# A slot table and the order of VectorE's work in the two mixer stages of a two-layer transformer kernel

## The reference, cut to what matters

```python
# block 1: mixer M0
q_a, k_a, v_a, q_b, k_b, v_b, g_a, g_b = split(rms(x) @ w_in)
y_a = moba_attention(rotary(q_a), rotary(k_a), v_a)       # 8 softmax heads
y_b = stick_breaking_attention(q_b, k_b, v_b)             # 8 heads, log-sigmoid sums
merged = sigmoid(g_a + b) * (y_a @ w_branch_moba) + sigmoid(g_b + b) * (y_b @ w_branch_sb)
x = x + merged @ w_out
# block 2: mixer M1
fq, fk, fv, ff, dq, dk, dv, iq, ik, iw, ga, gb = split(rms(x) @ w_in_2)
o_a = fox_attention(norm(fq), norm(fk), fv, log_sigmoid(ff + b_forget))   # 8 heads
score = sum_h iw[h] * relu(iq[h] . ik)                    # 8 index heads
sel = top_k(causal(score), 64)
o_b = dsa_attention(norm(dq), norm(dk), dv, sel, rel_bias)                # 8 heads
merged = sigmoid(ga) * (o_a @ w_branch_a) + sigmoid(gb) * (o_b @ w_branch_b)
x = x + merged @ w_out_2
```

## Time and profile before

| | us |
|---|---|
| median of three runs | 1149.95 (1149.85 to 1151.63) |
| the profiled execution's own time | 1151.63 |
| its span, first to last instruction | 1149.8 |
| PE busy | 1132.0 (98% of the span) |
| DVE busy | 691.5 (60%) |
| ACT busy | 577.7 (50%) |
| POOL busy | 66.0 (6%) |
| mean granted TensorE clock | 0.997 |

### The profile page before, as it was taken

The page is one execution under the profiler, slowest core; times in us unless marked ns, Lnnn a source line. Parts: engine busy times, 40 slices in busy tenths (PEclk is TensorE's granted clock), DMA queues, the critical chain, the costliest instruction groups (busy, mean ns, idle before and its releaser), DMA issues.

```text
span 1149.8 us, 13571 instructions
## 1 busy us (share of the span) xinstructions
PE 1132.0 (98%) x5422; PEld 943.1 (82%) x5422; DVE 691.5 (60%) x869; ACT 577.7 (50%) x714; POOL 66.0 (6%) x106
## 2 busy tenths in 40 slices
PE   8999999999999999999999999999899999999998
PEld 6888888888888888888888888888688888888887
DVE  5555554654887765555485555457995486555542
ACT  4444442667656444444354445337667764444440
POOL 2000000100000000000000000030344200000000
PEclk8999999999999999999999999999999999999999
DMA  9656566644445566555565555556634355555550
GB/s 310 224 183 186 184 225 214 200 164 144 141 174 176 172 201 191 184 192 183 183 201 183 184 183 183 195 164 239 201 112 146 127 168 180 186 183 183 183 183 37
DMA packets 143039, 208.53 MB, mean 181 GB/s; under 512 B 9336, under 2 KB 100616, under 8 KB 142976
## 3 DMA queue, kind: packets, MB, share of 16 engines
q1 hardware_dynamic: 139296, 198.01, 52.7%
q0 software_dynamic: 3248, 9.06, 2.3%
q10 hardware_dynamic: 432, 0.59, 0.2%
HBM read 206.56 MB, written 2.64 MB: 182 GB/s over the span
## 4 chain that ended last, share of the span: by engine, by line
PE 90%; DVE 4%; ACT 3%; issue 1%; DMA 1%; SPq 0%; ACTq 0%; DVEq 0%
PE bank L1526 28%; PE bank L1528 27%; PE bank L1527 27%; PE bank L1635 2%; DVE w_lo L1041 2%; DMA raw<-in_ffn_w_up 1%; ACT w_hi L710 1%; PE bank L1548 1%; PE bank L1765 1%; PE bank L1792 1%; PE bank L1793 1%; DVE stat L1406 1%; PE bank L1791 0%; PE bank L1752 0%; DVE gate L1364 0%
## 5 line engine op out<-in xcount | busy, mean ns | idle before, releaser
L1041 DVE TENSOR_TENSOR w_lo<-raw,w_hi 128x2048 fp32r<-128x2048 f32 (+1 forms) x187 | 426.1, 2283 | 215.5 <-ACT w_hi L710 215.2
L1526 PE MATMUL bank<-w_hi,xT_hi 128*128 128x512 f32 (+1 forms) x1112 | 440.1, 396 | 1.8 <-DVE xT_lo L1061 1.8
L1528 PE MATMUL bank<-w_hi,xT_lo 128*128 128x512 f32 (+1 forms) x1112 | 432.9, 389 | 0.0
L1527 PE MATMUL bank<-w_lo,xT_hi 128*128 128x512 f32 (+1 forms) x1112 | 431.9, 388 | 0.0
L710 ACT ACTIVATE w_hi<-raw 128x2048 fp32r<-128x2048 f32 (+1 forms) x187 | 354.7, 1901 | 109.2 <-PE bank L1528 105.1
L1528 PEld LDWEIGHTS bank<-w_hi,xT_lo 128*128 128x128 f32 x1112 | 209.1, 188 | 44.5
L1526 PEld LDWEIGHTS bank<-w_hi,xT_hi 128*128 128x128 f32 x1112 | 209.4, 188 | 41.1 <-DVE w_lo L1041 2.0
L1527 PEld LDWEIGHTS bank<-w_lo,xT_hi 128*128 128x128 f32 x1112 | 209.7, 189 | 39.7
L1526 PE MATMUL bank<-w_hi,hT_hi 128*128 128x512 f32 x352 | 137.7, 391 | 0.0
L1528 PE MATMUL bank<-w_hi,hT_lo 128*128 128x512 f32 x352 | 137.1, 389 | 0.0
L1527 PE MATMUL bank<-w_lo,hT_hi 128*128 128x512 f32 x352 | 137.0, 389 | 0.0
(11 more groups left out here) (274 smaller groups left out, 780.7 us busy)
## 6 DMA issues: line engine op xcount, KB each, us to landing
raw<-in_ffn_w_gate SPq DMA_DIRECT2D x88, 512.0 KB, 4.0
raw<-in_ffn_w_up SPq DMA_DIRECT2D x88, 512.0 KB, 5.0
raw<-in_ffn_w_down SPq DMA_DIRECT2D x88, 512.0 KB, 4.2
raw<-in_w_in SPq DMA_DIRECT2D x76, 512.0 KB, 4.5
raw<-in_w_out SPq DMA_DIRECT2D x16, 512.0 KB, 4.0
raw<-in_w_branch_moba SPq DMA_DIRECT2D x4, 512.0 KB, 5.0
raw<-in_w_branch_sb SPq DMA_DIRECT2D x4, 512.0 KB, 6.0
raw<-in_w_branch_a SPq DMA_DIRECT2D x4, 512.0 KB, 4.5
```

The costliest lines, as they stand in the source:

```text
L1041: dve.tensor_tensor(w_lo[r][:, 0:n], raw[r][:, 0:n], w_hi[u % SLOTS][:, 0:n], ALU.subtract).then_inc(lo_done, 1)
L1526: pe.matmul(dst, st(hi), mhi, start=start, stop=False)
L1527: pe.matmul(dst, st(hi), mlo, start=False, stop=False)
L1528: return pe.matmul(dst, st(lo), mhi, start=False, stop=stop)
```

## The change

The edit moves work between slots and within a slot. No instruction on data is added or taken away by the source. For M0 the DVE part of each slot now has `gate_rows` first and `sb_keep` behind the `split_lo`. For M1 the index heads stand one per slot at 10 to 17 and their `accumulate` is two slots after the scores, ahead of the split. The transposes of fk and fq come up to two slots later and in another order, dk's at slot 28, the fox heads at 21 and 23 to 29, dq's at 30 and 31, and the dsa heads at 32 to 39. The second `norm_heads` moves to slot 19, `norm_dk` to 18, the top rounds to slots 20 to 27, `select` to 28 and 29.

```diff
-        out = [(6, "TR", ("iq", 0)), (7, "TR", ("iq", 1)), (9, "TR", ("ik", 0)), (12, "CU", ())]
-        out += [(t, "IX", h) for h, t in enumerate((10, 10, 11, 11, 12, 13, 13, 14))]
-        out += [(16, "TR", ("fq", 0)), (17, "TR", ("dk", 0)), (18, "TR", ("fq", 1))]
-        out += [(19, "TR", ("fk", 0)), (20, "TR", ("fk", 1))]
-        out += [(t, "SM", ("fox", h)) for h, t in enumerate((21, 22, 23, 24, 25, 26, 27, 28))]
-        out += [(29, "TR", ("dq", 0)), (30, "TR", ("dq", 1))]
-        out += [(t, "SM", ("dsa", h)) for h, t in enumerate((31, 32, 33, 34, 35, 36, 37, 38))]
+        out = [(6, "TR", ("iq", 0)), (7, "TR", ("iq", 1)), (9, "TR", ("ik", 0)), (11, "CU", ())]
+        out += [(10 + h, "IX", h) for h in range(NH)]
+        out += [(18, "TR", ("fq", 0)), (19, "TR", ("fk", 0)), (20, "TR", ("fq", 1)), (22, "TR", ("fk", 1))]
+        out += [(t, "SM", ("fox", h)) for h, t in enumerate((21, 23, 24, 25, 26, 27, 28, 29))]
+        out += [(28, "TR", ("dk", 0)), (30, "TR", ("dq", 0)), (31, "TR", ("dq", 1))]
+        out += [(t, "SM", ("dsa", h)) for h, t in enumerate((32, 33, 34, 35, 36, 37, 38, 39))]
...
-                rounds = {17 + k: k for k in range(TOPK // 8)}
+                rounds = {20 + k: k for k in range(TOPK // 8)}
...
+                    if b == 0 and q == 0 and 7 <= j <= 10:
+                        dve.wait_ge(tri_done, 1)
+                        gate_rows(j - 1)
                     for it in ITEMS[b]:
...
-                        if it.kind == "SB" and d == SB_AT["keep"]:
-                            sb_keep(it)
                         if it.kind == "SM" and d == SM_AT["out"]:
                             invert(it)
-                    if b == 0 and q == 0 and 7 <= j <= 10:
-                        dve.wait_ge(tri_done, 1)
-                        gate_rows(j - 1)
+                        if it.kind == "IX" and d == 2:
+                            accumulate(it)
...
-                        if slot == 16:
-                            norm_heads(0)
-                            norm_dk()
+                        if slot in (16, 19):
+                            norm_heads((slot - 16) // 3)
                     if q in (1, 3) and 1 < slot < 42:
                         for u in next_units(ph, j)[q // 2:q // 2 + 1]:
                             split_lo(u)
...
                         if slot == 18:
-                            norm_heads(1)
+                            norm_dk()
...
-                        if it.kind == "IX" and d == 1:
-                            accumulate(it)
+                        if it.kind == "SB" and d == SB_AT["keep"]:
+                            sb_keep(it)
...
-                    if b == 1 and slot in (25, 26):
-                        select(slot - 25)
+                    if b == 1 and slot in (28, 29):
+                        select(slot - 28)
```

## The result

The changed kernel takes 1156.82 us (median of 4 runs, 1155.52 to 1158.11) where the kernel before takes 1150.02 (median of 4, 1149.85 to 1151.63). The ratio is 1.0056, with a 95% interval of 1.0038 to 1.0074: some 6.4 us (0.0056 x 1150) slower. The profiled execution took 1156.88, with a span of 1155.1. The forecast was 1154.5 within 1150.8 to 1157.6, slower with a chance of 0.70.

A forecast was written before the change was run, and what follows sets the result against it. The prediction took PE to bound the kernel. M0 +3.8 and M1 -3.8 + 4.5 = +0.7 gave +4.5 us, taking the median from 1149.95 to 1154.5; own range 1153.0 to 1156.3, 8-in-10 range 1150.8 to 1157.6.

The forecast's parts named there:

- M0, DVE and ACT queues: M0's first two stick-breaking heads: the new order makes PE wait 1.4, then 2.4 us, together 3.8 us later.
- M1 body: M1, index heads to fox heads: PE's waits shrink from 6.9 to 3.5 us; gain taken as 3.8.
- M1 tail: End of M1: the last dsa head's exponentials fall behind the Sigmoid preload, adding two table loads; 4.5 us lost.
- the first step: M0, first head: keep behind the split makes PE's sum wait and the next scores start 1.4 us later.
- its step: M0, second head: `gate_rows` ahead of the clamp delays softplus and `w_hi`; PE's second sum waits 2.3 to 2.4 us more.
- Up to 816 us the spread work fits in gaps: M1: the index heads' accumulates stand where DVE waited for `w_hi`; DVE's last idle moment is at 816.2.
- the walk: M1: DVE's queue followed by row durations from 816.2, 28.1 us of work, to fk1's `turn_rest` ending at 844.3.
- Missing loads: Rival, M1's tail: the table loads don't come or don't hold PE; tail loses 1.9, total 1151.9; chance 0.15.
- M0's first step only: Rival, M0: the order costs only its first step, 1.4 us, total 1152.1; chance 0.10.
- a cleared backlog: Rival, M1: DVE's backlog clears wholly, 1146.8, or 1149.4 with loads; chance 0.10 under 1147.6, otherwise 0.05.
- M1 gains nothing: Rival, M1: the stalls don't shrink at all, total 1158.2; chance 0.10.
- the last two rivals: M1's stalls don't shrink, 1158.2, chance 0.10; a table load costs the page's price, 1157.3, chance 0.03.

The follow-up runs named there:

- after_again: The changed kernel itself, unaltered, executed once more for a second trace: 1156.79 us.
- m0_keep_only: The kernel before with only M0's `sb_keep` moved behind the split, `gate_rows` left in its old place: ratio 1.0019 to the kernel before.
- m1_part_no_masks: The changed kernel with M0's old order put back and each of POOL's eight masks cut to one column: ratio 1.0001 to the kernel before.
- m1_dsa_early_2: The kernel of m1_dsa_early run again, unaltered: ratio 0.9985 to the kernel before.
- m1_one_load: The changed kernel with M0's old order and M1's Sigmoid preload moved from slot 40 to behind slot 41's exponentials: ratio 0.9993 to the kernel before.
- m0_part_only: The kernel before with both M0 moves (`gate_rows` first, `sb_keep` behind the split) and M1 as before: ratio 1.0045 to the kernel before.
- m1_dsa_early: The changed kernel with M0's old order, and dq's transposes and the dsa heads at their old slots: ratio 0.9988 to the kernel before.
- the kept-busy kernel: m0_part_only with useless matmuls on PE ahead of the first two sums, their results overwritten: ratio 1.0032 to the kernel before.
- m0_gate_only: The kernel before with only M0's `gate_rows` moved ahead of the items, `sb_keep` left ahead of the split: ratio 1.0023 to the kernel before.
- m1_early_dk_late: m1_dsa_early with `norm_dk` moved to slot 24, behind fox's four transposes: ratio 0.9997 to the kernel before.

## Why the prediction was right, and where it was off

| step | forecast | measured in the trace after |
|---|---|---|
| M0, DVE and ACT queues | +3.8 | +3.82 (3.75 in after_again) |
| M0, clock | none | +1.6 here, 0 in after_again |
| M1 body | -3.8 | -2.95 |
| M1 tail | +4.5 | +4.6 |
| sum | +4.5 | +7.05 |

The measured 1156.82 lies inside the stated range, but 0.5 above the forecast's own 1153.0 to 1156.3. Part of the nearness is luck: the profiled execution, forecast at 1156.1, took 1156.88 because it started 1.8 us early; with before's start the same work would have ended at 1151.63 + 7.05 = 1158.7.

**M0's queues: right.** The second sum stands 311.25 - 309.25 + 1.82 = 3.82 later, for the start's 1.82. Of the first step, 0.97 was forecast for the first sum, and 0.97 it was. More than half of the third wait is the doing of `gate_rows`, as its step said: counted from the first sum, the second keep ends at 311.15 - 300.83 = 10.3 in the changed kernel and at 309.84 - 300.84 = 9.0 in m0_keep_only, with `gate_rows` back in its place. That m0_keep_only shows no third wait at all is the slow clock's doing.

**M0's clock: missing.** No term of the sum stood for what PE's clock does behind a wait. Before, PE has no waits over 0.3 us in this stretch, and in M1, where it has four of 0.9 to 2.3, the clock is 1.00 in that trace: from there I could read that waits are harmless, and read it too generally. That the waits bring the fall is shown: in all six traces with new waits in M0 the clock fell there once, and in the other eight, with M0's old order or with PE kept busy in the first and third wait, it stayed at 1.00. This is the largest error, 1.6 us.

**M1's body: the mechanism right, the size off.** POOL's masks do "start some 4 us earlier" and "are over by then": they end ahead of `norm_dk`. The step that failed is "Up to 816 us the spread work fits in gaps", with DVE's last idle moment at 816.2. It priced the masks for `norm_dk` alone and left everything that they now fell on at its old duration. They start 3.8 us earlier against PE's work (16.67 us after the first index scores, in place of 20.44), but `norm_heads` of slot 16 is only 1.6 us earlier (17.06 in place of 18.67). It had run ahead of the masks and now runs among them: 4.3 us (814.91 to 819.19) in place of 1.85. `norm_dk` escaped them, as forecast (0.65, near the lower bound of 0.7), and the rest was hit: the accumulate 1.71 in place of 0.74, the split 2.71. So the contention moved and did not go. DVE has no idle moment there, and the split of slot 17 starts at 820.93 - 3.53 = 817.40 on before's scale, 1.2 us after the walk's 816.2 (3.53 is how much later M1's first index scores stand in this trace); without the masks, in m1_part_no_masks, it starts at 816.6 on that scale. The waits add up to 4.2 (0.35, 1.81, 0.43, 1.61) where 3.5 was forecast, and fk0's, forecast at 0.5, is the one that is off. The end of fk1's `turn_rest` is at 848.91 - 3.53 = 845.4, 1.1 us later than the 844.3 of the walk; no wait followed it, where 0.4 was forecast. m1_part_no_masks gives 1.2 us back, and m1_dsa_early_2 shows what else it hangs on: there the DMA that feeds the masks landed a microsecond later, the 128x18 instructions kept their 0.18, and fk0's wait was 1.06 where the same kernel had 1.92.

The Trainium skill (SBUF — State Buffer, section "SBUF: two separate sides") says that a GpSimd operation and a DVE operation with two SBUF inputs exclude each other on a shared port pair, for the whole instruction. The rows fit: a DVE instruction of 0.18 with two such inputs takes up to 0.67 beside masks of 0.87 each, and in m1_dsa_early_2 the reduce with one input (820.72, 1.21 us) keeps its time beside masks that run to 822.09. By that rule, overlap with POOL should have been priced for every DVE instruction with two SBUF inputs in the masks' 7 us, not for `norm_dk` alone.

**M1's tail: right.** The 4.6 of the table is 16.09 - 10.61 less the 0.85 of PE's work that the forecast also took off, and the body is what is left of M1's 1.7. Three loads, PE's waits before the last turn (1.83, "about 2") and before `y_turn` (2.40, "2 to 3"), +16.09 where +15.95 was forecast. The drain that the Trainium skill (ScalarE: Activation LUTs, section "What ACT_TABLE_LOAD costs") gives for a load does not show: 917.31 follows 916.01 + 1.28 at once, as the earlier trace rows showed, and m1_one_load's 2.86 for two loads leaves 0.15 each for all that is around them.

**The rivals.** Missing loads, M0's first step only, and a cleared backlog are all excluded by the trace. That M1 gains nothing is excluded too, though the body gained 0.85 less. The total came nearer to the last two rivals (1158.2 and 1157.3) than to the forecast, but for another reason than theirs, mostly the clock: M1's waits did shrink, and two loads cost 2.86, hardly more than 2 x 1.28.

**Still open.** What decides where the clock falls. In M0 it fell behind the same three waits at one of two places. In M1 it fell in five of the fourteen traces, each time about the first of the longer waits (1.9 to 2.3 us): in m0_part_only and m0_keep_only, whose M1 is that of the kernel before, in after_again, m1_one_load and m1_dsa_early. It cost nothing there (interval B 127.34 and 127.38 in the first two, where before has 127.34), since more waits follow. No kernel here was made to find what sets it. The price by run times alone is not sharp either: the kept-busy kernel's 1.5 us lies within the two intervals, and it is the traces (intervals A of 497.02 and 495.42 for one kernel, 495.48 with PE kept busy) that carry it.

## What to carry to other kernels

Walk each queue with the rows' durations: the walk gave M0's queues and the tail to 0.15 us. Then ask two more questions of it: which of the moved instructions now lie under another engine's work on the same memory, and whether a new wait of a microsecond or two on an otherwise full PE is followed by a stretch at half clock. An operation on an in-order list that switches a table belongs behind the last user of the old table, and a half that gains should be kept when the other loses: here M1's new order with the dsa heads and M0 left alone runs at 0.9985 to 0.9988 of the kernel before, the best of all that ran: a gain of 1.4 to 1.7 us, small, with intervals that end just under 1.

## What the runs showed of the hardware

- PE's granted clock fell to 0.50 behind two waits of 0.80 and 0.71 us (m0_keep_only, after_again), behind a further one of 2.17 (after, m0_part_only), and behind a single one of 1.95 (m0_gate_only); behind M1's 2.29 it did not in the trace of before, and did in m0_part_only, which has the same M1. 128x512 matmuls take 0.63 us then in place of 0.39 and start 0.43 apart in place of 0.23. A fall is worth 1.6 us if no wait follows (after, m0_gate_only), some 0.6 where about 1.0 would have been waited anyway (m0_keep_only, an estimate), and nothing if waits that long follow (after_again, m0_part_only in M1).
- The place of the fall is not a property of the program: the same kernel had it at 304 to 308 us in one execution and at 311 to 315 in another (after_again, after).
- DVE instructions stretch beside POOL's: 128x18 from 0.18 to 0.67, the 128x512 pair from 1.29 to 2.33, the scaling of dk's rows from 0.42 to 1.48, the split from 2.29 to 2.71 and 2.85 (after and m1_early_dk_late).
- A table load takes 1.28 us, and the next operation starts at once (917.31 behind 916.01 + 1.28 in after); two loads taken out of the tail brought its end 2.86 us earlier, 1.43 each (m1_one_load).
